# One product for two 16-key tiles in an attention's value products

## The chip, the cores and the metric

The kernel runs on one core of a Trainium2 chip. TensorE (PE) multiplies, VectorE (DVE) and ScalarE (ACT) do elementwise work, GpSimd (POOL) some sums and DMA issues, SyncE (SP) issues the loads of weights. The metric is the time of one execution in device microseconds.

## The reference

One layer of a hybrid decoder in float32: 512 tokens of 1024 features with 16 meta tokens in front (T = 528). Attention (16 heads of 64) and a causal convolution module (31 taps) read the same normalised input; their gated sum goes through an output projection, then come a squared-ReLU MLP and a last normalisation. The change touches only the attention:

```
logit[t,s] = q_t.k_s/sqrt(64) + sum_{s<j<=t} log f_j        (s <= t)
starts = [0] + list(range(16, 528, 128))
block [q0,q1) reads keys [0,q1):  p = softmax(s);  out = p @ v[:, :q1]
```

The outputs of the meta tokens' own block are dropped, so there are four query tiles of 128 queries, q = 0 to 3, with 144, 272, 400 and 528 keys.

## The kernel before

**Precision.** Every float32 operand of a large product is held as a high and a low part in float32r (`*_hi`, `*_lo`). A projection's chunk is 8 x 3 products (high by high, low by high, high by low). Its weights are copied to `w_hi` by ACT (L568) and the rest to `w_lo` by DVE (L940).

**Pairs and steps.** Heads are worked in 8 pairs. A pair takes 8 steps, `s` = 0 to 7; step `s` handles unit `s`: head `s // 4` of the pair and query tile `s % 4`. At the same time PE computes the next pair's four projections (v, gate, q, k; one chunk in two steps), so that the products of a chunk stand between the pieces of attention work. DVE fills its time with the taps of the convolution (L1035), a fixed number in each step (`TAPS_STEP`, 18 or 19 in a pair; pairs 5 to 8 have the extra one in step 4). The order on every engine is written out by hand (`pair_step`), engines meet by semaphores.

**A unit.** PE multiplies queries by keys into PSUM (`unit_scores`, L1544, L1545); DVE adds the mask, writes `prob` and takes the row's minimum (L1075); ACT exponentiates with a row sum (L657); DVE takes the reciprocal (L1081); ACT normalises `prob` in place (`normalise`, L665). One step later PE transposes `prob` in tiles of 128 keys (`unit_transpose`, L1558); ACT copies the result to `pt_hi` (L673, `probs_high`) and DVE the rest to `pt_lo` (L1087, `probs_low`). The transposes of a unit wait for the previous unit's low part (`s_ptl`) and for the unit's own normalisation (`s_pn`).

**Tiles of keys.** 144 + 128 q keys make q + 2 tiles, the last of which has 16 keys. It lies in `prob` in a cell of 128 columns whose other columns are zero (`pads`), so that it is transposed like the others; `v_hl`, v's transposed high and low parts, has five tiles, the fifth with 16 keys and zeros.

**Values.** After two units, `half_out` multiplies: v's tile is stationary, the transposed probabilities of two query tiles move, 256 columns. A half has query tiles 0 and 1 (half 0) or 2 and 3 (half 1). The last tile of the half's second query tile stands alone: its products have 128 columns (L1578), the others 256 (L1575). Half 0 is in steps 3 (head 0) and 7 (head 1), half 1 in step 5 and in step 1 of the next pair, each behind the transposes of its step. ACT's copy of unit 2 or 6 to `pt_hi` waits for half 0 (`s_pv`).

**v.** In step 3 ACT copies the next pair's v product to `vT` (L693), in the same step as it normalises unit 3; PE transposes `vT` in step 2 of the next pair and writes the PSUM of `vT`'s product again from step 4 on, for which it waits (`s_vev`).

Of the kernel before, what the change touches and what calls it, by code (L numbers as in the profile page):

```python
# [20 lines left out]
F32 = mybir.dt.float32  # L21
F32R = mybir.dt.float32r
ALU = mybir.AluOpType
ACT = mybir.ActivationFunctionType
AX_X = mybir.AxisListType.X

P = 128
D = 1024
KT = D // P
NT = 512  # L30
META = 16
T = NT + META
H = 16
HD = 64
PAIRS = H // 2
QT = NT // P
# [54 lines left out]
KT5 = QT + 1  # L91
VT = KT5 * P
SHORT_AT, LONG_AT = 0, 4 * P
FIRST_CELL = (0, 2, 0, 4)
CELLS = 9
N_F = 2
N_GLU = 1
N_PAIR = N_GLU + 2 * KT
# [26 lines left out]
def build(nc, x, meta_tokens, norm_mix_gain, w_in, b_forget, w_attn_out, b_glu, conv_dw_w, conv_dw_b,  # L125
# [3 lines left out]
    with ExitStack() as ctx:  # L129
        def sb(name, shape, dt=F32):  # L130
            return ctx.enter_context(nc.sbuf_tensor(name, shape, dt))

        def sem(name):
            return ctx.enter_context(nc.semaphore(name))
# [18 lines left out]
        ga = sb("ga", [P, KT * NT])  # L153

        in_hi = sb("in_hi", [P, KT * ROW], F32R)
        in_lo = sb("in_lo", [P, KT * ROW], F32R)

        with ExitStack() as pairs_only:  # L160
            k_a, k_b, q_a, q_b = (pairs_only.enter_context(nc.sbuf_tensor(name, [P, 2, 2, width], F32R))
                                  for name, width in (("k_a", T), ("k_b", T), ("q_a", NT), ("q_b", NT)))
            pt_hi, pt_lo = (pairs_only.enter_context(nc.sbuf_tensor(name, [P, CELLS * P], F32R))
                            for name in ("pt_hi", "pt_lo"))
            v_hl = pairs_only.enter_context(nc.sbuf_tensor("v_hl", [P, KT5, 2, P], F32R))
# [6 lines left out]
        pT = sb("pT", [P, 2, NT])  # L172
        sb("rest_pt", [P, 2 * CELLS * P - 2 * NT])
        xs_meta_t = sb("xs_meta", [P, D])
# [4 lines left out]
        vT = sb("vT", [P, VT])  # L179
        ident = sb("ident", [P, P])  # L180
# [1 line left out]
            d_lo = last_block.enter_context(nc.sbuf_tensor("d_lo", [P, KT * NT], F32R))  # L182
        u = sb("u", [P, KT * UW])
        prm = sb("prm", [P, KT * NR])
        ones = sb("ones", [P, 1])
        nmax = sb("nmax", [P, 8])
        rsum = sb("rsum", [P, 8])
        rinv = sb("rinv", [P, 8])
        eps_rms = sb("eps_rms", [P, 1])
        eps_ln = sb("eps_ln", [P, 1])  # L190
        bf = sb("bf", [H, 1])
        ss = sb("ss", [P, 2 * QT])
        sd = sb("sd", [P, QT + 1])
        rstd = sb("rstd", [P, QT + 1])
# [2 lines left out]
        pj = ctx.enter_context(nc.psum_tensor("pj", [P, 2, 1024], F32))  # L197
# [3 lines left out]
        pO7 = pQ[:, 1536:2048]  # L201
# [28 lines left out]
        def probs(q, first=0, last=None):  # L230

            end = LONG_AT if q % 2 == 0 else LONG_AT + VT
            at = end - (q + 2) * P
            return prob[:, at + first:end if last is None else at + last]

        def turned(q):

            at = 1024 - (P if q == QT - 1 else 0)
            return pQ[:, at:at + (q + 2) * P]

        def cells(buf, q):

            return buf[:, FIRST_CELL[q] * P:(FIRST_CELL[q] + q + 2) * P]

        def count(k, it=None, per=0):

            return k if it is None else it * per + k

        def wait(eng, signal, k, it=None, per=0):

            if it is None and k <= 0:
                return
            assert k > 0
            eng.wait_ge(signal, count(k, it, per))
# [5 lines left out]
        def feat(buf, m):  # L260
            return buf[:, ds(m * NT, NT)]
# [8 lines left out]
        AT = 512 - HALF  # L270

        def prod(c, width=NT):
            if width == T:
                return pj[:, c % 2, AT:AT + T]
            return pj[:, 0, 0:NT] if c % 2 == 0 else pj[:, 1, 512:512 + NT]

        HW = D // 2
        down_hi = (d_hi[:, :], in_hi[:, 0:KT * HW])  # L280
# [10 lines left out]
        def y_psum(t, f):  # L291

            return (pQ if f == 0 else pj[:, :, :].rearrange("p a b -> p (a b)"))[:, t * HW:(t + 1) * HW]
# [48 lines left out]
        s_vev = sem("s_vev")  # L342
# [14 lines left out]
        s_one = sem("s_one")  # L357
# [21 lines left out]
        s_pn = sem("s_pn")  # L379
# [181 lines left out]
        def _(act):  # L561
            A = nc.scalar.activation
# [97 lines left out]
            def normalise(s, k, it=None):  # L660

                U = 8 * k + s
                wait(act, s_rinv, U + 1, it, 16)
                nk = META + P * (s % QT + 1)
                A(probs(s % QT, 0, nk), probs(s % QT, 0, nk), ACT.Copy, scale=rinv[:, s:s + 1]).then_inc(s_pn, 1)  # L665

            def probs_high(s, k, it=None):

                U = 8 * k + s
                h, q = divmod(s, QT)  # L670
                wait(act, s_T, U + 1, it, 16)
                wait(act, s_pv, 4 * k + 2 * h + q // 2, it, 8)
                A(cells(pt_hi, q), turned(q), ACT.Copy).then_inc(s_pth, 1)  # L673
# [12 lines left out]
            def projection_out(s, k, it=None):  # L686

                c = N_PAIR + 4 * k + s // 2
                if s == 3:
                    if k == 0:  # L690
                        act.wait_ge(s_u, KT + 1)
                    wait(act, s_vl, k, it, 2)
                    A(vT[:, 0:T], prod(c - 1, T), ACT.Copy).then_inc(s_vev, 1)  # L693
                elif s % 2 == 0 and c > N_PAIR:
                    wait(act, s_mm, c, it, 8)
                    if s == 0:
                        A(feat(ga, count(k - 1, it, 2)), prod(c - 1), ACT.Copy).then_inc(s_gev, 1)
                    elif s in (4, 6):
                        dst, width, scale, done = (q_a, NT, -HD ** -0.5, s_qh) if s == 4 else (k_a, T, 1.0, s_kh)
                        for h in range(2):  # L700
                            A(dst[0:HD, k % 2, h, :], prod(c - 1, width)[h * HD:(h + 1) * HD, :], ACT.Copy,
                              scale=scale).then_inc(done, 1)
# [74 lines left out]
            for s in range(8):  # L777
                k = PAIRS
                c = N_PAIR + 4 * k + s // 2
# [14 lines left out]
            for k in (PAIRS + 1,):  # L794
                for s in range(8):
                    c = N_PAIR + 4 * k + s // 2
# [137 lines left out]
        def _(dve):  # L934
            V = nc.vector
# [20 lines left out]

            V.memset(f_one, 1.0).then_inc(s_one, 1)
            V.memset(vT[:, T:VT], 0.0).then_inc(s_one, 1)
            for cell in (3, 8):
                V.memset(pads[:, cell, META:P], 0.0).then_inc(s_pads, 1)  # L960
            V.memset(q_b[HD:HD + 2, :, :, :].bitcast(F32), -1.0).then_inc(s_one2, 1)
# [121 lines left out]
            def probs_low(s, k):  # L1083

                q = s % QT
                wait(dve, s_pth, 8 * k + s + 1)
                V.tensor_tensor(cells(pt_lo, q), turned(q), cells(pt_hi, q).bitcast(F32),  # L1087
                                ALU.subtract).then_inc(s_ptl, 1)
# [167 lines left out]
            for m in range(KT):  # L1256
                c = N_AO + m
# [11 lines left out]
            with dve.Fori(0, KT // 4) as it:  # L1269
                for j in range(4):  # L1270
                    m = it * 4 + j
                    c = N_CO + j
# [138 lines left out]
        def _(pe):  # L1411
            mm = nc.tensor.matmul
# [94 lines left out]
            for m in range(KT):  # L1507
                last = nc.tensor.transpose(pPrm[:, m * NR:(m + 1) * NR], prow[:, m * P:(m + 1) * P],
                                           ident[0:NR, 0:NR])
# [39 lines left out]
            def unit_transpose(s, k, it=None):  # L1549

                U = 8 * k + s
                q = s % QT
                wait(pe, s_pn, U + 1, it, 16)
                wait(pe, s_ptl, U, it, 16)
                if q == QT - 1 and U + 2 <= 8 * PAIRS:
                    wait(pe, s_max, U + 2, it, 16)
                for t in range(q + 2):
                    last = nc.tensor.transpose(turned(q)[:, t * P:(t + 1) * P], probs(q, t * P, (t + 1) * P), ident[:, :])  # L1558
                last.then_inc(s_T, 1)

            def half_out(h, half, k, it=None):

                q0 = 2 * half
                wait(pe, s_ptl, 8 * k + 4 * h + q0 + 2, it, 16)
                if half == 0:
                    wait(pe, s_vl, k + 1, it, 2)
                    wait(pe, s_ob, 2 * k + h, it, 4)
                dst = pO7[:, q0 * P:(q0 + 2) * P]
                for t in (0, q0 + 2, *range(1, q0 + 2)):
                    for part in (pt_hi, pt_lo):  # L1570
                        grid = part[:, :].rearrange("p (c n) -> p c n", n=P)
                        first, second = FIRST_CELL[q0] + t, FIRST_CELL[q0 + 1] + t
                        flags = dict(start=t == 0 and part is pt_hi, stop=t == q0 + 1 and part is pt_lo)
                        if t < q0 + 2:
                            last = mm(dst.rearrange("p (c n) -> p c n", n=P), v_hl[:, t, h, :],  # L1575
                                      grid[:, first:second + 1:second - first, :], **flags)
                        else:
                            last = mm(dst[:, P:2 * P], v_hl[:, t, h, :], grid[:, second, :], **flags)  # L1578
                last.then_inc(s_pv, 1)

            def values_transpose(k, it=None):
# [43 lines left out]

            pe.wait_ge(s_sig, KT + 1)
            pe.wait_ge(s_one2, 1)
            pe.wait_ge(s_one, 2)
            pe.wait_ge(s_pads, 2)
            for k in range(2):  # L1630
                for s in range(8):
# [20 lines left out]
            for n0, hi, lo, ready in ((N_AO, mid_hi, mid_lo, s_olo), (N_CO, in_hi, in_lo, s_clo)):  # L1652
                with pe.Fori(0, KT // 4) as it:
                    for j in range(4):
                        begin(n0 + j, it)
                        chunk(n0 + j, 0, total, hi, lo,
                              first=(lambda kt: pe.wait_ge(ready, kt + 1)) if j == 0 else None)
# [69 lines left out]
            for f in range(2):  # L1727
                for t in range(QT):
# [6 lines left out]
                    for kt in range(KT):  # L1735
# [4 lines left out]
                        for hidden, w, n in ((mid_hi, down_hi, 0), (mid_hi, down_lo, 1), (mid_lo, down_hi, 2)):  # L1740
                            last = mm(y_psum(t, f), hidden[:, tok], w[f][:, cols],  # L1741
                                      start=kt == 0 and n == 0, stop=kt == KT - 1 and n == 2)
# [29 lines left out]
```

## Time and profile before

| | us |
|---|---|
| three runs | 914.67, 916.97, 917.04 |
| median | 916.97 |
| the profiled execution | 913.51 |
| its span | 911.5 |
| PE, DVE, ACT busy in it | 901.0, 612.5, 443.7 |

The span runs from the first to the last instruction that the profiler recorded. Attention's eight pairs stand between about 135 and 405 us; before them are the convolution's gate projections, behind them the output projections and the MLP, in which PE does almost only products of 512 columns.

### The profile page before, as it was taken

What the parts mean: (1) busy time and instruction counts of PE and PEld (TensorE: products, weight loads), DVE (VectorE), ACT (ScalarE), POOL (GpSimd) and SP (SyncE); (2) the same over time, 40 slices, a digit from 0 to 9 for tenths busy, and PEclk for the clock granted to TensorE, in tenths of its full rate; (3) what the DMA queues carried; (4) which work ended last, traced back from release to release, by engine and by line L of the source; (5) the groups of instructions that cost most, each with busy time, mean ns of one, the idle gap of its engine ahead of it and who ended that gap; (6) DMA issues with size and microseconds to landing.
All of it is one profiled execution on the core that took longest, in us unless ns stands there. A gap on an engine that the chain in (4) does not pass through costs nothing.

```text
span 911.5 us, 13692 instructions
## 1 busy us (share of the span) xinstructions
PE 901.0 (99%) x5045; PEld 785.5 (86%) x5045; DVE 612.5 (67%) x956; ACT 443.7 (49%) x720; POOL 22.3 (2%) x40
## 2 busy tenths in 40 slices
PE   8999999999999999999999999999999999999997
PEld 7999998899999999888888888888888888888886
DVE  7699989999999999986766444533443354334543
ACT  6432246777778777766842244421243133214423
POOL 2010000000000000010000000000000000000000
PEclk9999999999999999999999999999999999999999
DMA  9333332212221222212323532333233332333502
GB/s 263 96 97 93 91 94 70 70 49 70 69 66 50 69 70 56 80 56 87 115 79 104 186 93 83 102 93 101 86 103 104 92 92 93 114 93 108 169 1 93
DMA packets 129466, 84.34 MB, mean 93 GB/s; under 512 B 3103, under 2 KB 118815, under 8 KB 129424
## 3 DMA queue, kind: packets, MB, share of 16 engines
q1 hardware_dynamic: 128192, 82.32, 30.9%
q10 hardware_dynamic: 640, 1.18, 0.4%
q8 instruction: 25, 0.41, 0.2%
q0 software_dynamic: 592, 0.29, 0.2%
q14 instruction: 17, 0.14, 0.0%
HBM read 81.62 MB, written 2.16 MB: 92 GB/s over the span
## 4 chain that ended last, share of the span: by engine, by line
PE 94%; DVE 3%; ACT 1%; issue 1%; DMA 1%; ACTq 0%; DVEq 0%
PE pj L1435 42%; PE pQ L1675 19%; PE pj L1431 17%; PE pQ L1558 3%; PE pQ L1575 3%; PE pj L1741 2%; PE pQ L1741 2%; PE pj L1473 1%; DVE cv L1035 1%; PE pQ L1545 1%; PE pQ L1544 1%; DVE w_lo L940 1%; PE pQ L1578 1%; DMA u<-in_norm_mix_gain_dram 1%; PE pQ L1452 1%
## 5 line engine op out<-in xcount | busy, mean ns | idle before, releaser
L940 DVE TENSOR_TENSOR w_lo<-raw,w_hi 128x1024 fp32r<-128x1024 f32 x129 | 157.7, 1222 | 114.6 <-ACT w_hi L568 114.2
L568 ACT ACTIVATE w_hi<-raw 128x1024 fp32r<-128x1024 f32 x129 | 135.9, 1053 | 161.4 <-PE pQ L1675 121.3
L1435 PE MATMUL pj<-in_hi,w_lo 128*128 128x512 f32 x512 | 201.5, 393 | 0.0
L1435 PE MATMUL pj<-in_lo,w_hi 128*128 128x512 f32 x512 | 200.7, 392 | 0.0
L1435 PE MATMUL pj<-in_hi,w_hi 128*128 128x512 f32 x512 | 200.6, 392 | 0.0
L1035 DVE SCALAR_TENSOR_TENSOR cv<-u,prm,cv 128x512 f32<-128x512 f32 x240 | 170.6, 745 | 0.5
L1435 PEld LDWEIGHTS pj<-in_hi,w_hi 128*128 128x128 f32 x512 | 96.3, 188 | 20.4 <-DVE w_lo L947 0.9
L1435 PEld LDWEIGHTS pj<-in_lo,w_hi 128*128 128x128 f32 x512 | 96.2, 188 | 18.0 <-issue 0.2
L1435 PEld LDWEIGHTS pj<-in_hi,w_lo 128*128 128x128 f32 x512 | 96.3, 188 | 17.1
L1675 PE MATMUL pQ<-w_hi,mid_hi 128*128 128x512 f32 x256 | 99.8, 390 | 0.0
L1675 PE MATMUL pQ<-w_lo,mid_hi 128*128 128x512 f32 x256 | 99.6, 389 | 0.0
L1675 PE MATMUL pQ<-w_hi,mid_lo 128*128 128x512 f32 x256 | 99.6, 389 | 0.0
L1431 PE MATMUL pj<-in_hi,w_lo 128*128 128x264 f32 x480 | 97.9, 285 | 0.0
L1431 PE MATMUL pj<-in_lo,w_hi 128*128 128x264 f32 x480 | 97.4, 284 | 0.0
L1431 PE MATMUL pj<-in_hi,w_hi 128*128 128x264 f32 x480 | 96.7, 283 | 0.4 <-ACT vT L693 0.4
L1431 PEld LDWEIGHTS pj<-in_hi,w_hi 128*128 128x128 f32 x480 | 74.9, 188 | 1.6 <-issue 0.7
L1431 PEld LDWEIGHTS pj<-in_lo,w_hi 128*128 128x128 f32 x480 | 74.0, 188 | 0.0
L1431 PEld LDWEIGHTS pj<-in_hi,w_lo 128*128 128x128 f32 x480 | 73.9, 188 | 0.0
L881 ACT ACTIVATE prob<-pT 128x512 f32<-128x512 f32 x32 | 20.2, 632 | 102.3 <-DVE pT L1326 102.3
L657 ACT ACTIVATE prob<-prob,nmax 128x144 f32<-128x144 f32 (+1 forms) x64 | 36.7, 573 | 42.0 <-DVE nmax L1075 42.0
L1675 PEld LDWEIGHTS pQ<-w_hi,mid_lo 128*128 128x128 f32 x256 | 48.1, 188 | 10.0
L1675 PEld LDWEIGHTS pQ<-w_lo,mid_hi 128*128 128x128 f32 x256 | 48.1, 188 | 10.0
(197 smaller groups left out, 1236.3 us busy)
## 6 DMA issues: line engine op xcount, KB each, us to landing
raw<-in_w_in_dram SPq DMA_DIRECT2D x57, 512.0 KB, 3.8
raw<-in_w_mlp_up_dram SPq DMA_DIRECT2D x32, 512.0 KB, 3.9
raw<-in_w_mlp_down_dram SPq DMA_DIRECT2D x32, 512.0 KB, 3.8
raw<-in_w_attn_out_dram SPq DMA_DIRECT2D x8, 512.0 KB, 3.6
raw<-in_w_conv_out_dram SPq DMA_DIRECT2D x8, 512.0 KB, 3.6
raw<-in_w_out_dram SPq DMA_DIRECT2D x8, 512.0 KB, 3.9
ga<-in_x_dram SPq DMA_DIRECT2D x4, 512.0 KB, 8.8
cv<-in_x_dram SPq DMA_DIRECT2D x1, 2048.0 KB, 9.1
```

Source lines behind the costliest of these rows:

```text
L568: A(w_hi[:, c % SPLIT, :], raw[:, c % RAW, :], ACT.Copy).then_inc(s_hi, 1)
L657: A(probs(s % QT, 0, nk), probs(s % QT, 0, nk), ACT.Exp, bias=nmax[:, s:s + 1], scale=-1.0, accum_out=rsum[:, s:s + 1]).then_inc(s_exp, 1)
L881: A(scratch(j), pT[:, j % 2, :], ACT.Square).then_inc(s_hf, 1)
L940: V.tensor_tensor(w_lo[:, c % SPLIT, :], raw[:, c % RAW, :], w_hi[:, c % SPLIT, :].bitcast(F32), ALU.subtract).then_inc(s_lo, 1)
L1035: V.scalar_tensor_tensor(out=dst, in0=src, scalar=par(j, m), in1=dst, op0=ALU.mult, op1=ALU.add).then_inc(s_conv, 1)
L1431: last = mm(prod(c, T)[:, h * HALF:(h + 1) * HALF], wt, src[:, kt * ROW + FIRST + h * HALF:kt * ROW + FIRST + (h + 1) * HALF], **flags)
L1435: last = mm(prod(c), wt, src[:, at:at + NT], **flags)
L1452: last = nc.tensor.transpose(in_psum(t)[:, m, :], src, ident[0:n, 0:n])
L1558: last = nc.tensor.transpose(turned(q)[:, t * P:(t + 1) * P], probs(q, t * P, (t + 1) * P), ident[:, :])
L1575: last = mm(dst.rearrange("p (c n) -> p c n", n=P), v_hl[:, t, h, :], grid[:, first:second + 1:second - first, :], **flags)
L1675: last = mm(y_psum(t, 0), mid[:, tok], w[:, c % SPLIT, cols], start=kt == 0 and n == 0, stop=kt == KT - 1 and n == 2)
L1741: last = mm(y_psum(t, f), hidden[:, tok], w[f][:, cols], start=kt == 0 and n == 0, stop=kt == KT - 1 and n == 2)
```

## The change

The lone tiles of query tiles 1 and 3 are multiplied together, one product for the high and one for the low part, in half 1. Both need one stationary operand, so the fifth tile of `vT` holds keys 256 to 271 in rows 0 to 15 and keys 512 to 527 in rows 32 to 47. Query tile 1's lone tile has its keys in rows 0 to 15 already; query tile 3's are put in rows 32 to 47, by normalising them into a new buffer `lone_probs` of 48 columns, 32 of them zero, from which the last transpose of the unit reads. The product takes 48 rows and moves 256 columns (cells 4 and 9 of `pt_hi` or `pt_lo`). `FIRST_CELL` gives query tile 3 cells 5 to 9, so that query tile 1's lone cell outlives the copies of units 2 and 3. The accumulation of a head is now started once, in half 0, for all four query tiles.

ACT's `normalise` has two instructions for query tile 3, and its copy of v has two. The new buffer takes free columns in front of the rows of `in_lo`; four one-column constants move into one tensor; DVE zeroes 32 columns more at the start.

```diff
...
 KT5 = QT + 1
 VT = KT5 * P
 SHORT_AT, LONG_AT = 0, 4 * P
-FIRST_CELL = (0, 2, 0, 4)
-CELLS = 9
+FIRST_CELL = (0, 2, 0, 5)
+CELLS = 10
+LONE_ROW = 32
 N_F = 2
 N_GLU = 1
 N_PAIR = N_GLU + 2 * KT
...
         ga = sb("ga", [P, KT * NT])
 
         in_hi = sb("in_hi", [P, KT * ROW], F32R)
+        with ExitStack() as row_gap:
+            lone_probs = row_gap.enter_context(nc.sbuf_tensor("lone_probs", [P, LONE_ROW + META], F32))
         in_lo = sb("in_lo", [P, KT * ROW], F32R)
 
 
...
             d_lo = last_block.enter_context(nc.sbuf_tensor("d_lo", [P, KT * NT], F32R))
         u = sb("u", [P, KT * UW])
         prm = sb("prm", [P, KT * NR])
-        ones = sb("ones", [P, 1])
         nmax = sb("nmax", [P, 8])
         rsum = sb("rsum", [P, 8])
         rinv = sb("rinv", [P, 8])
-        eps_rms = sb("eps_rms", [P, 1])
-        eps_ln = sb("eps_ln", [P, 1])
-        bf = sb("bf", [H, 1])
+        columns = sb("columns", [P, 4])
+        ones, eps_rms, eps_ln = (columns[:, i:i + 1] for i in range(3))
+        bf = columns[0:H, 3:4]
         ss = sb("ss", [P, 2 * QT])
         sd = sb("sd", [P, QT + 1])
         rstd = sb("rstd", [P, QT + 1])
...
             at = end - (q + 2) * P
             return prob[:, at + first:end if last is None else at + last]
 
+        def probs_cell(q, t):
+            return lone_probs[:, :] if (q, t) == (QT - 1, QT) else probs(q, t * P, (t + 1) * P)
+
         def turned(q):
 
             at = 1024 - (P if q == QT - 1 else 0)
...
             return pj[:, 0, 0:NT] if c % 2 == 0 else pj[:, 1, 512:512 + NT]
 
 
+
+        def lone_values(c):
+
+            at = AT + 2 * P
+            return pj[:, c % 2, at:at + 4 * P].rearrange("p (a b) -> p a b", b=2 * P)[:, :, 0:META]
 
         HW = D // 2
         down_hi = (d_hi[:, :], in_hi[:, 0:KT * HW])
...
                 U = 8 * k + s
                 wait(act, s_rinv, U + 1, it, 16)
                 nk = META + P * (s % QT + 1)
-                A(probs(s % QT, 0, nk), probs(s % QT, 0, nk), ACT.Copy, scale=rinv[:, s:s + 1]).then_inc(s_pn, 1)
+                last = A(probs(s % QT, 0, min(nk, NT)), probs(s % QT, 0, min(nk, NT)), ACT.Copy, scale=rinv[:, s:s + 1])
+                if nk > NT:
+                    last = A(lone_probs[:, LONE_ROW:], probs(s % QT, NT, nk), ACT.Copy,
+                             scale=rinv[:, s:s + 1])
+                last.then_inc(s_pn, 1)
 
             def probs_high(s, k, it=None):
 
...
                     if k == 0:
                         act.wait_ge(s_u, KT + 1)
                     wait(act, s_vl, k, it, 2)
-                    A(vT[:, 0:T], prod(c - 1, T), ACT.Copy).then_inc(s_vev, 1)
+                    A(vT[:, 0:NT], prod(c - 1, T)[:, 0:NT], ACT.Copy)
+                    A(vT[:, NT:VT].rearrange("p (a b) -> p a b", b=LONE_ROW)[:, 0:2, 0:META],
+                      lone_values(c - 1), ACT.Copy).then_inc(s_vev, 1)
                 elif s % 2 == 0 and c > N_PAIR:
                     wait(act, s_mm, c, it, 8)
                     if s == 0:
...
 
             V.memset(f_one, 1.0).then_inc(s_one, 1)
             V.memset(vT[:, T:VT], 0.0).then_inc(s_one, 1)
+            V.memset(lone_probs[:, 0:LONE_ROW], 0.0).then_inc(s_one, 1)
             for cell in (3, 8):
                 V.memset(pads[:, cell, META:P], 0.0).then_inc(s_pads, 1)
             V.memset(q_b[HD:HD + 2, :, :, :].bitcast(F32), -1.0).then_inc(s_one2, 1)
...
                 if q == QT - 1 and U + 2 <= 8 * PAIRS:
                     wait(pe, s_max, U + 2, it, 16)
                 for t in range(q + 2):
-                    last = nc.tensor.transpose(turned(q)[:, t * P:(t + 1) * P], probs(q, t * P, (t + 1) * P), ident[:, :])
+                    last = nc.tensor.transpose(turned(q)[0:probs_cell(q, t).shape[1], t * P:(t + 1) * P], probs_cell(q, t),
+                                               ident[:, :])
                 last.then_inc(s_T, 1)
 
             def half_out(h, half, k, it=None):
...
                 if half == 0:
                     wait(pe, s_vl, k + 1, it, 2)
                     wait(pe, s_ob, 2 * k + h, it, 4)
-                dst = pO7[:, q0 * P:(q0 + 2) * P]
-                for t in (0, q0 + 2, *range(1, q0 + 2)):
+                dst = pO7.rearrange("p (c n) -> p c n", n=P)
+                for t in (0, 1) if half == 0 else (0, QT, 1, 2, 3):
                     for part in (pt_hi, pt_lo):
                         grid = part[:, :].rearrange("p (c n) -> p c n", n=P)
-                        first, second = FIRST_CELL[q0] + t, FIRST_CELL[q0 + 1] + t
-                        flags = dict(start=t == 0 and part is pt_hi, stop=t == q0 + 1 and part is pt_lo)
-                        if t < q0 + 2:
-                            last = mm(dst.rearrange("p (c n) -> p c n", n=P), v_hl[:, t, h, :],
-                                      grid[:, first:second + 1:second - first, :], **flags)
+                        if t < QT:
+                            first, second = FIRST_CELL[q0] + t, FIRST_CELL[q0 + 1] + t
+                            last = mm(dst[:, q0:q0 + 2, :], v_hl[:, t, h, :], grid[:, first:second + 1:second - first, :],
+                                      start=half == 0 and t == 0 and part is pt_hi,
+                                      stop=t == QT - 1 and part is pt_lo)
                         else:
-                            last = mm(dst[:, P:2 * P], v_hl[:, t, h, :], grid[:, second, :], **flags)
+                            first, second = FIRST_CELL[1] + 2, FIRST_CELL[QT - 1] + t
+                            rows = LONE_ROW + META
+                            mm(dst[:, 1:QT:2, :], v_hl[0:rows, t, h, :], grid[0:rows, first:second + 1:second - first, :],
+                               start=False, stop=False)
                 last.then_inc(s_pv, 1)
 
             def values_transpose(k, it=None):
...
 
             pe.wait_ge(s_sig, KT + 1)
             pe.wait_ge(s_one2, 1)
-            pe.wait_ge(s_one, 2)
+            pe.wait_ge(s_one, 3)
             pe.wait_ge(s_pads, 2)
             for k in range(2):
                 for s in range(8):
```

## Rows read from the trace of the kernel before

**Rows 1.** The page: busy us (share, count) by engine; chain's shares
```profile
PE 901.0 (99%) x5045; PEld 785.5 (86%) x5045; DVE 612.5 (67%) x956; ACT 443.7 (49%) x720; POOL 22.3 (2%) x40
...
PE 94%; DVE 3%; ACT 1%; issue 1%; DMA 1%; ACTq 0%; DVEq 0%
```
**Rows 2.** Windows: stretch, its length, busy us by engine, clock, DMA
```profile
242.81:275.60 32.79, 32.79 (x230) 30.35 (x229) 30.79 (x63) 24.60 (x49) 1.81 (x2) 1.00 0.23 64
275.60:308.53 32.93, 32.93 (x230) 30.32 (x229) 31.34 (x64) 24.62 (x49) 1.83 (x2) 1.00 0.23 64
```
**Rows 3.** Groups by form: busy us, mean ns of one, idle before
```profile
L1575 PE MATMUL pQ<-pt_lo,v_hl 128*128 128x256 f32 x96 | 25.7, 282 | 0.0
...
L1578 PE MATMUL pQ<-pt_lo,v_hl 128*128 128x128 f32 x32 | 8.8, 275 | 0.0
...
L1578 PE MATMUL pQ<-pt_hi,v_hl 128*128 128x128 f32 x32 | 7.2, 224 | 0.0
```
**Rows 4.** Timeline of weight loads, step 3 of pair 4: start us, us
```profile
248.44 0.19 PEld L1575 LDWEIGHTS pQ<-pt_hi,v_hl 128*128 128x128 f32 x1
...
248.67 0.19 PEld L1578 LDWEIGHTS pQ<-pt_hi,v_hl 128*128 128x128 f32 x1
248.78 0.19 PEld L1578 LDWEIGHTS pQ<-pt_lo,v_hl 128*128 128x128 f32 x1
248.90 0.19 PEld L1575 LDWEIGHTS pQ<-pt_hi,v_hl 128*128 128x128 f32 x1
```
**Rows 5.** Timeline of PE where 48 stationary columns follow 128
```profile
27.32 0.64 PE L1473 MATMUL pj<-in_hi,w_lo 128*128 128x264 f32 x4
27.80 0.28 PE L1484 MATMUL pj<-in_hi,w_hi 128*48 128x264 f32 x1
```
**Rows 6.** Timeline of PE before unit 4's transposes: pairs 4, 5 and 1
```profile
255.83 0.41 PE L1431 MATMUL pj<-in_lo,w_hi 128*128 128x264 f32 x2
256.08 0.38 PE L1558 MATMUL pQ<-ident,prob 128*128 128x128 f32 x2
...
288.58 0.40 PE L1431 MATMUL pj<-in_lo,w_hi 128*128 128x264 f32 x2
288.90 0.41 PE L1558 MATMUL pQ<-ident,prob 128*128 128x128 f32 x2
...
157.60 0.41 PE L1558 MATMUL pQ<-ident,prob 128*128 128x128 f32 x2 [0.23 <-DVE pt_lo L1087]
```
**Rows 7.** Timeline of ACT, steps 3 and 4 of pair 4
```profile
248.18 0.59 ACT L693 ACTIVATE vT<-pj 128x528 f32<-128x528 f32 x1
248.67 0.72 ACT L665 ACTIVATE prob<-prob,rinv 128x528 f32<-128x528 f32 x1
249.45 0.60 ACT L673 ACTIVATE pt_hi<-pQ 128x512 fp32r<-128x512 f32 x1
249.94 1.05 ACT L568 ACTIVATE w_hi<-raw 128x1024 fp32r<-128x1024 f32 x1
```
**Rows 8.** Timeline of DVE, minima of steps 3 and 5, pair 4
```profile
246.69 0.71 DVE L1075 CUSTOM_DVE_ANT_0 prob<-pQ,mask 128x528 f32<-128x528 f32 x1 [0.75 <-PE pQ L1545]
...
254.58 0.44 DVE L1075 CUSTOM_DVE_ANT_0 prob<-pQ,mask 128x272 f32<-128x272 f32 x1 [0.46 <-PE pQ L1545]
```
**Rows 9.** Timeline of DVE: pair 5's steps 4 and 5, pair 1's step 4
```profile
286.12 1.41 DVE L1125 SCALAR_TENSOR_TENSOR q_a<-pj,q_a 64x512 fp32r<-64x512 f32 x2
287.57 0.44 DVE L1075 CUSTOM_DVE_ANT_0 prob<-pQ,mask 128x272 f32<-128x272 f32 x1
287.93 0.09 DVE L1075 DVE_READ_ACCUMULATOR2_ANT nmax<- 128x1 f32 x1
287.93 0.82 DVE L1087 TENSOR_TENSOR pt_lo<-pQ,pt_hi 128x640 fp32r<-128x640 f32 x1
...
153.98 0.16 DVE L1081 RECIPROCAL rinv<-rsum 128x1 f32<-128x1 f32 x1 [0.27 <-ACT prob L657]
```
**Rows 10.** Groups by form on ACT; PE's waits: us, times, longest
```profile
L665 ACT ACTIVATE prob<-prob,rinv 128x528 f32<-128x528 f32 x16 | 11.7, 733 | 2.2 <-DVE rinv L1081 2.2
...
L665 ACT ACTIVATE prob<-prob,rinv 128x144 f32<-128x144 f32 x16 | 6.5, 406 | 1.2 <-DVE rinv L1081 1.2
...
PE pj L1431 <- ACT vT L693: 0.4, 1, 0.4
```

## The prediction

> **What bounds the kernel now.** I read the page first. TensorE (PE) is busy for 901.0 of 911.5 us and holds 94% of the chain that ended last [rows 1]. The change lies in the attention pairs, so next come the windows of two of the eight pairs (each from one transpose of v to the next): PE is never idle, its clock is at full speed, VectorE (DVE) works 30.8 and 31.3 us of 32.8 and 32.9, ScalarE (ACT) 24.6 [rows 2]. So PE sets the pace, but DVE is close: a fraction of a microsecond saved on PE can turn into a wait for DVE. What I have to find is the price of the removed products on PE, and which waits of a pair have no slack.
>
> **The price of a product.** The durations of [rows 3] overlap and are no price; starts are. In the loads around the products of one half, that of the first lone product starts at 248.67, of the second at 248.78, of the next 256-wide one at 248.90 [rows 4]: 0.11 and 0.12 us each, so the lone pair takes 0.23 us. The 256-wide ones go at 0.12 (248.44 to 248.67 is two of them, 0.23). So a product of 128 columns costs as much as one of 256: the weight load in front of it (0.11 us apart at best) is what it pays for.
>
> **Part by part, PE.** Per head four products of 128 columns go (q1's and q3's, high and low part; 64 in all [rows 3], which shows 32 of either part) and two of 256 columns with 48 rows come. Removed 4 x 0.115 = 0.46, added 2 x 0.12 = 0.24: 0.22 us less per head, 16 heads, 3.5 us at most. By place: the first half of a head (in steps 3 and 7 of a pair) becomes 0.23 shorter, the second half (steps 5 and 1 of the next) 0.01 longer. That a product of 48 rows costs what one of 128 does is my value, since no row shows 48; the ends are 0.11 for each, the shortest spacing of [rows 4] (0.3 us more gain in all), and the rival with the drain below. The last transpose of query tile 3 now has 48 stationary columns, still 128 moving ones. Going from 128 to 48 stationary columns costs nothing in the start of the kernel: four products from 27.32 at 0.12 put the fourth at 27.68, and the first 48-column one starts at 27.80 [rows 5]. I take 0 for it; ends 0.05 us either way for each of 16 (half of the 0.11 of a load), so 0.8.
>
> **Part by part, ACT.** The normalisation of query tile 3 becomes two instructions (512 and 16 wide), 16 times; v's copy becomes two (512, and 2 x 16), 8 times. From 128x144 at 406 ns and 128x528 at 733 [rows 10], an element costs 0.85 ns and an instruction 284 ns fixed; 16 wide makes about 0.30 us. But v's copy (0.59 long) starts 0.49 before the instruction behind it, 248.18 to 248.67 [rows 7]: about 0.10 of each duration overlaps. So a tail costs ACT 0.20 us, less the 0.014 taken from the wide part: 0.19; for v's, reading PSUM, I take 0.10. Ends: 0 and 0.30 for each. Total about 3.8 us of ACT's, which works 24.6 of 32.8, so only its place matters.
>
> In step 3 the order is exponential, v's copy, normalise(3), then the high copy of unit 2's turned probabilities, then w_hi, q's copies, exponential(4) and its row sum, on which DVE's reciprocal waits. Now normalise(3) starts at 248.67 and the copy behind at 249.45, 0.78 later, though 0.62 would do (0.72 less 0.10) [rows 7]: 0.16 is a wait for the first half's products, which will end 0.23 sooner. Tails of 0.29 less 0.16 leave ACT about 0.13 late from there to the reciprocal (ends 0 and 0.4).
>
> **What PE's saving then meets.** Steps 3 to 5 are the tight place. DVE starts from step 3's scores after idling 0.75, and works through to step 5's row minimum, behind which stands the low part of unit 3, on which unit 4's transposes on PE wait.
> - Pairs 2 to 4 (such as the one at 242.81): DVE idles 0.46 before step 5's minimum [rows 8], and PE starts the transposes 0.25 after the last but one product, 255.83 to 256.08 [rows 6], the ordinary spacing of two 264-wide products. PE 0.23 earlier and DVE 0.13 later make 0.36 of 0.46: it fits. Saving 2 x 0.22 per pair, three pairs: 1.3 us.
> - Pairs 5 to 7 have one conv tap more in step 4. DVE goes from there into the minimum at 287.57 without idling [rows 9], and PE waits: 288.58 to 288.90 is 0.32, 0.07 over the ordinary [rows 6]. The first head's 0.22 is lost whole, and ACT's 0.13 comes on top; the second head's 0.22 stays (the chain has 0.75 idle in front of the next step 3, of which 0.22 goes). 0.09 per pair, 0.3 us.
> - Pair 1: PE idles on DVE's low part already, at 157.60 [rows 6], and in its step 4 DVE waits for ACT 0.27, at 153.98 [rows 9], so the whole 0.29 of the tails comes through. Its second head saves 0.22: net -0.07.
> - Pair 8 has no q and v left to cast and no such wait that I see: 0.44.
> - PE waits once for v's copy, 0.4 us, in the first step [rows 10]: a longer copy adds 0.1.
>
> In step 7 the tail of normalise(7) delays exponential and reciprocal of the next step by 0.2; DVE takes that from its 0.75. Memsets at the start stand beside DMA waits; the merged constants and the shifted buffers cost nothing (DVE and PE do not touch them differently). SP's and POOL's queues get nothing new, and the new value of PE's start wait is long reached.
>
> Sum: 1.3 + 0.3 - 0.1 + 0.4 - 0.1 = 1.9 us (with all rounding, ends 0 and 3.5). The profiled execution took 913.51 us for a span of 911.5: it would become 911.6. The three runs go from 914.67 to 917.04, median 916.97; the sum taken from the median gives 915.1, and I say 915.0, since the profiled execution and one run lie below.
>
> **A rule weighed.** That the load, not the columns, prices the lone products is what the starts show [rows 4]. The Trainium skill, "TensorEngine Tiling (Array Packing)", Key Properties, speaks against the change: in its words "Mode switching requires drain", and it gives row tiling for contractions of at most 64 rows, where these have 48. In columns, this trace does not agree ([rows 5], 0.12 us across the switch). In rows, no run here shows it yet; it is the second rival.
>
> **The rivals.**
> 1. All is kept. The waits in steps 4 and 5 turn out looser (the tails on ACT nearly free, DVE's order giving way elsewhere). For it: the waits that I see are under 0.1 us each in pairs 5 to 7. Against: an engine without idle time cannot move up. Gain 3.5: 913.5.
> 2. A change of rows drains PE. A product's result lasts 282 ns [rows 3] and the next starts 0.12 after it; if the array must be empty before 48-row weights act, and again after, each of two changes per head costs 0.28 - 0.12 = 0.16, 32 of them 5.2 us. 5.2 - 1.9 = 3.3 slower: 920.3. It decides from 0.06 us per change on. For it: nothing of these rows shows 64 rows or fewer beside full products without a wait. Against: 128 to 48 columns is free [rows 5]. Place: the loads of the two 48-row products, in steps 5 and 1.
> 3. ACT's tails are dear (0.3 each, not hidden). The copy behind them comes 0.6 - 0.16 = 0.44 late. Pairs 2 to 4 then wait too, 0.23 + 0.44 - 0.46 = 0.21 each, and still save 0.23 (0.7 in all); pairs 5 to 7 lose 0.22 each (0.7), pair 1 loses 0.4, pair 8 saves 0.4, the first step loses 0.3. In sum about 0: 917.0. For it: a tail is almost all fixed cost. Against: the overlap of 0.10 is seen behind every ACT row of [rows 7].
>
> **Chances.** Forecast (gain 1 to 2.9) 0.53; rival 1 0.18; rival 3 0.15; rival 2 0.12; other 0.02. What a measurement can tell from no change is 0.3%, 2.75 us. Faster by more than that: rival 1 nearly whole, a tenth of the forecast's, and scatter of the median: 0.27. Slower: rival 2 mostly, 0.11. Within: 0.62. The range goes from 912.4 (3.5 gained, and a median 1 us low) to 918.0 (rival 3 with a median 1 us high); rival 2 is left out.
>
> **What would show it.** In the profile after: 32 products of 256 columns with 48 rows in place of 64; starts 0.12 apart around them (0.28 would be rival 2); first halves 0.23 shorter; pairs 2 to 4 about 32.35 us long, pairs 5 to 7 about 32.85; PE's wait before unit 4's transposes in pairs 5 to 7 about 0.4 us instead of 0.07; DVE's idle 0.46 fallen to 0.1; the tail on ACT 0.30 us long. I am wrong if pairs 5 to 7 shorten as much as 2 to 4 (rival 1), or if all of them lengthen.

## The result and the profile after

The changed kernel is slower: 917.81 us (median of 15 runs, 917.45 to 920.67) against 914.56 for the kernel before, run beside it (15 runs, 913.14 to 917.04). The ratio is 1.0037, 95% interval 1.0027 to 1.0048. In most kernels here some runs, with a mean granted clock of 0.992 to 0.994 instead of 0.996 to 1.000, take 2 to 4 us longer, so that a median also depends on how many of them it holds. The forecast was 915.0 with most of the chance on "within 0.3%"; what came has the sign and the size of its second rival (3.3 us slower), the size in part by luck (see the part on why the prediction was wrong). The profiled execution took 918.48 us with a span of 916.5, 5.0 us over the span before; about 0.6 of that is there before the first unit's transposes. In the first 15 us TensorE (PE) waits for the first inputs (0.7 us for DVE cv and 1.3 for xs_meta, 0.4 and 0.8 before) and its granted clock is 0.89, 1.00 before; this start differs by up to 1 us between the kernels here.

The page, busy us by engine and the chain's shares, answering to [rows 1]:

```profile
PE 903.9 (99%) x5013; PEld 783.4 (85%) x5013; DVE 613.6 (67%) x957; ACT 446.4 (49%) x744; POOL 22.3 (2%) x40
...
PE 91%; DVE 4%; ACT 3%; issue 1%; DMA 1%; ACTq 0%; DVEq 0%
```

32 products less, and yet PE's time is longer: what has grown lies between products. DVE and ACT have gained shares of the chain. The windows of pairs 4 and 5 against [rows 2] put 0.39 and 0.63 us on a pair, with the clock still at full speed:

```profile
245.07:278.25 33.18, 33.18 (x227) 30.14 (x226) 30.91 (x63) 24.92 (x52) 1.82 (x2) 1.00 0.23 64
278.25:311.81 33.56, 33.34 (x227) 30.15 (x226) 31.54 (x64) 24.94 (x52) 1.84 (x2) 1.00 0.23 63
```

The weight loads of a second half (step 5 of pair 4), to be read by their starts, as [rows 4]:

```profile
258.30 0.19 PEld L1592 LDWEIGHTS pQ<-pt_lo,v_hl 128*128 128x128 f32 x1
258.63 0.18 PEld L1598 LDWEIGHTS pQ<-pt_hi,v_hl 48*128 48x128 f32 x1
258.74 0.19 PEld L1598 LDWEIGHTS pQ<-pt_lo,v_hl 48*128 48x128 f32 x1
259.06 0.19 PEld L1592 LDWEIGHTS pQ<-pt_hi,v_hl 128*128 128x128 f32 x1
```

Here is the loss. The first load with 48 rows starts 0.33 behind the load before it, the second 0.11 behind the first, and the first with 128 rows again 0.32 behind: the ordinary spacing is 0.11 to 0.12. All 16 second halves show the same, 0.32 or 0.33 at either change. A change of rows, in either direction, costs about 0.2 us. The timeline of PE shows the same from the side of the products: starts 0.21 and 0.22 apart, in place of 0.12, though the products are of the ordinary width:

```profile
258.42 0.28 PE L1592 MATMUL pQ<-pt_lo,v_hl 128*128 128x256 f32 x1
258.63 0.38 PE L1598 MATMUL pQ<-pt_hi,v_hl 48*128 48x256 f32 x1
258.85 0.28 PE L1598 MATMUL pQ<-pt_lo,v_hl 48*128 48x256 f32 x1
```

The groups by form show it only on the first product behind a change: the high part's with 48 rows is 382 ns long, the low part's 277, beside 281 for the low part's with 128 rows and [rows 3]. The two tails on ScalarE (ACT), the short second instructions, are the others of the new rows:

```profile
L1598 PE MATMUL pQ<-pt_hi,v_hl 48*128 48x256 f32 x16 | 6.1, 382 | 0.0
L677 ACT ACTIVATE lone_probs<-prob,rinv 128x16 f32<-128x16 f32 x16 | 4.7, 295 | 0.0
...
L1598 PE MATMUL pQ<-pt_lo,v_hl 48*128 48x256 f32 x16 | 4.4, 277 | 0.0
...
L708 ACT ACTIVATE vT<-pj 128x32 f32<-128x32 f32 x8 | 1.5, 186 | 0.0
```

The second loss is the one that the prediction had for pairs 5 to 7. PE before unit 4's transposes in pair 5, as [rows 6]: the last but one product starts at 291.00, the transposes at 291.62, 0.62 instead of 0.32, and the ordinary is 0.25:

```profile
291.00 0.40 PE L1448 MATMUL pj<-in_lo,w_hi 128*128 128x264 f32 x2
291.62 0.41 PE L1575 MATMUL pQ<-ident,prob 128*128 128x128 f32 x2 [0.22 <-DVE pt_lo L1104]
```

And PE's waits, of which v's copy has grown from [rows 10]:

```profile
PE pQ L1575 <- DVE pt_lo L1104: 1.1, 4, 0.4
PE pj L1448 <- ACT vT L708: 0.7, 1, 0.7
```

### The profile page after: what moved, and what is told of

The parts are those of the page before. It is cut to its first block, busy times and chain, and to the rows that moved or that the text cites. A ratio compares the mean times of both kernels' runs of the same rounds, so it can differ in the third digit from the quotient of the medians.

```text
span 916.5 us, 13653 instructions
## 1 busy us (share of the span) xinstructions
PE 903.9 (99%) x5013; PEld 783.4 (85%) x5013; DVE 613.6 (67%) x957; ACT 446.4 (49%) x744; POOL 22.3 (2%) x40
## 4 chain that ended last, share of the span: by engine, by line
PE 91%; DVE 4%; ACT 3%; issue 1%; DMA 1%; ACTq 0%; DVEq 0%
PE pj L1452 41%; PE pQ L1696 19%; PE pj L1448 15%; PE pQ L1592 3%; PE pj L1762 2%; PE pQ L1762 2%; PE pQ L1575 2%; PE pj L1490 1%; DVE cv L1052 1%; PE pQ L1562 1%; PE pQ L1561 1%; PE pQ L1598 1%; ACT w_hi L578 1%; DVE w_lo L956 1%; DMA u<-in_norm_mix_gain_dram 1%
```

## The experiments

Each kernel ran beside the kernel before on the same chip, in three sets (medians of that 913.8 to 913.9). The changed kernel was in none of them, so a difference in us from its 917.81, or between two sets, can be off by some tenths; the ratios are each to the kernel before beside it. The letters A to E name theories: A is that a change of rows empties PE; the others are told in the expectations.

**All 128 rows.** The joined product stays; only its rows change.

```diff
-                            rows = LONE_ROW + META
+                            rows = P
```

> The changed kernel with all 128 rows in the two joint products (rows 48 to 127 of v's fifth tile are zero). Theory A, a change between products of 128 rows and of 48 empties TensorE: in the changed trace the load of the first 48-row product starts 0.32 us behind the load before it instead of 0.12, and so does the first 128-row one behind them, 0.20 us each, 32 times, 6.5 us. Then this kernel loses them: second halves at the ordinary spacing (10 products in about 1.18 us instead of 1.56), time 911.3 to 913.5, that is about 2 us under the kernel before, as the prediction's sum without its rival said. Theory B, the loss is in ScalarE's two tails and the waits behind them: time stays at about 917.8.

Measured 912.44 us, ratio 0.9984 (0.9974 to 0.9993). By the medians 5.4 us came back from one number. From the first unit's transposes to the last unit's PE takes 258.18 us before, 262.10 in the changed kernel and 256.44 here: 5.7 us for the 30 changes between, 0.19 for each. The same place in step 5 of pair 4, weight loads:

```profile
256.30 0.19 PEld L1592 LDWEIGHTS pQ<-pt_lo,v_hl 128*128 128x128 f32 x1
256.42 0.19 PEld L1598 LDWEIGHTS pQ<-pt_hi,v_hl 128*128 128x128 f32 x1
256.54 0.19 PEld L1598 LDWEIGHTS pQ<-pt_lo,v_hl 128*128 128x128 f32 x1
256.65 0.19 PEld L1592 LDWEIGHTS pQ<-pt_hi,v_hl 128*128 128x128 f32 x1
```

Both gaps are gone. Windows of pairs 4 and 5:

```profile
242.88:275.30 32.42, 32.42 (x227) 29.94 (x226) 30.85 (x63) 24.86 (x52) 1.81 (x2) 1.00 0.23 65
275.30:308.16 32.86, 32.66 (x227) 29.98 (x226) 31.38 (x64) 24.83 (x52) 1.83 (x2) 1.00 0.23 64
```

The prediction gave 32.35 and 32.85 for them, and 1.9 us for the whole, of which 1.7 came by the stretch above and 1.45 by the medians. So its sum holds for this kernel, and theory B falls.

**80 and 64 rows.** The same line with `rows = 80` and `rows = 64`.

> The same with 80 rows. Theory A with the limit at 64 rows (the part of the array that a product takes is counted in halves or wholes): no gap, as with 128 rows, 911.3 to 913.5. Theory A with a gap for any number of rows other than 128: loads 0.32 apart, 917.8. (The products with 66 rows in the scores show 0.12 and speak for the first.)

> The same with 64 rows. Theory A with the limit at 64 rows: gaps as with 48 rows, time as the changed kernel, 917.3 to 918.5. If 64 rows cost nothing: 911.3 to 913.5.

80 rows: 911.88 us, ratio 0.9978 (0.9966 to 0.9989). 64 rows: 917.90 us, 1.0048 (1.0032 to 1.0063). The loads of the joined products, 80 rows first, then 64:

```profile
256.37 0.19 PEld L1592 LDWEIGHTS pQ<-pt_lo,v_hl 128*128 128x128 f32 x1
256.50 0.19 PEld L1598 LDWEIGHTS pQ<-pt_hi,v_hl 80*128 80x128 f32 x1
```

```profile
257.54 0.19 PEld L1592 LDWEIGHTS pQ<-pt_lo,v_hl 128*128 128x128 f32 x1
257.87 0.18 PEld L1598 LDWEIGHTS pQ<-pt_hi,v_hl 64*128 64x128 f32 x1
```

0.13 against 0.33. Somewhere above 64 and at or below 66 rows the gap ends: the scores' products of 66 rows stand between full ones without it, 0.13 and 0.12 apart (step 3 of pair 5, 80-row kernel):

```profile
278.83 0.19 PEld L1561 LDWEIGHTS pQ<-k_a,q_a 128*128 128x128 f32 x1
278.96 0.19 PEld L1562 LDWEIGHTS pQ<-k_b,q_b 66*128 66x128 f32 x1
279.08 0.19 PEld L1452 LDWEIGHTS pj<-in_lo,w_hi 128*128 128x128 f32 x1
```

**The two products apart.** The order within a second half is changed, nothing else.

```diff
-                for t in (0, 1) if half == 0 else (0, QT, 1, 2, 3):
-                    for part in (pt_hi, pt_lo):
+                order = [(t, part) for t in ((0, 1) if half == 0 else (0, 1, 2, 3)) for part in (pt_hi, pt_lo)]
+                if half == 1:
+                    order.insert(2, (QT, pt_hi))
+                    order.insert(5, (QT, pt_lo))
```

> The changed kernel with the two 48-row products of a head apart: high part, then the two 128-row products of v's second tile, then the low part. Theory A, the price is paid at each change of rows: four changes per head instead of two, 32 more of 0.20 us, 6.4 us more than the changed kernel, about 924. Theory C, the price belongs to each 48-row product (it or its load is slow in itself): no difference, 917.8.

Measured 923.87 us, ratio 1.0115 (1.0096 to 1.0134), 6.1 over the changed kernel by the medians and 5.6 by the profiled spans (922.1 against 916.5). Step 5 of pair 4, weight loads; 0.33, 0.31, then 0.32 and 0.32:

```profile
260.09 0.19 PEld L1595 LDWEIGHTS pQ<-pt_lo,v_hl 128*128 128x128 f32 x1
260.42 0.18 PEld L1601 LDWEIGHTS pQ<-pt_hi,v_hl 48*128 48x128 f32 x1
260.73 0.19 PEld L1595 LDWEIGHTS pQ<-pt_hi,v_hl 128*128 128x128 f32 x1
260.84 0.19 PEld L1595 LDWEIGHTS pQ<-pt_lo,v_hl 128*128 128x128 f32 x1
261.16 0.18 PEld L1601 LDWEIGHTS pQ<-pt_lo,v_hl 48*128 48x128 f32 x1
261.48 0.19 PEld L1595 LDWEIGHTS pQ<-pt_hi,v_hl 128*128 128x128 f32 x1
```

As many products of 48 rows, twice as many changes, twice the gaps. The price is that of the change (A), not of the product (C).

**48 rows in the kernel before.** No joining, no tails, no new layout.

```diff
-                            last = mm(dst[:, P:2 * P], v_hl[:, t, h, :], grid[:, second, :], **flags)
+                            last = mm(dst[:, P:2 * P], v_hl[0:48, t, h, :], grid[0:48, second, :], **flags)
```

> The kernel before with its four lone products of a head taking 48 rows (16 hold keys, the others are zero) in place of 128, nothing else. Theory A: each of the two lone pairs of a head is a change and a change back, 64 changes at 0.205 us, 13 us more, about 927; the lone products stay 128 columns wide, so the price has nothing to do with joining two tiles. If the gap came from the joined product with its strided output: no difference, 914.

Measured 924.01 us, ratio 1.0113 (1.0094 to 1.0132): 10.2 us, not 13. The price of a change is confirmed without the joined product; its size was wrong on one side. Step 3 of pair 4:

```profile
252.34 0.19 PEld L1575 LDWEIGHTS pQ<-pt_lo,v_hl 128*128 128x128 f32 x1
252.66 0.18 PEld L1578 LDWEIGHTS pQ<-pt_hi,v_hl 48*128 48x128 f32 x1
252.77 0.19 PEld L1578 LDWEIGHTS pQ<-pt_lo,v_hl 48*128 48x128 f32 x1
253.03 0.19 PEld L1575 LDWEIGHTS pQ<-pt_hi,v_hl 128*128 128x128 f32 x1
```

Into the 48 rows it takes 0.32, out of them 0.26. Behind a product of 256 columns the load comes 0.21 late, behind one of 128 columns 0.15. It looks as if a load that changes the rows waits until the product in front of it is through, and a shorter one is through sooner: in the kernel before the product behind a 128-column one starts 0.06 after it (248.78 to 248.84 on PE), the one behind a 256-column one 0.12, the same 0.06 less. The wait itself is in no row, since the recorded ends of products are modelled. 32 x (0.21 + 0.15) = 11.5, near the 10.2 (10.5 by the spans, 922.0 against 911.5).

**The tails alone.** In the kernel before, query tile 3's normalisation and v's copy are cut in two.

```diff
-                A(probs(s % QT, 0, nk), probs(s % QT, 0, nk), ACT.Copy, scale=rinv[:, s:s + 1]).then_inc(s_pn, 1)
+                last = A(probs(s % QT, 0, min(nk, NT)), probs(s % QT, 0, min(nk, NT)), ACT.Copy, scale=rinv[:, s:s + 1])
+                if nk > NT:
+                    last = A(probs(s % QT, NT, nk), probs(s % QT, NT, nk), ACT.Copy, scale=rinv[:, s:s + 1])
+                last.then_inc(s_pn, 1)
...
-                    A(vT[:, 0:T], prod(c - 1, T), ACT.Copy).then_inc(s_vev, 1)
+                    A(vT[:, 0:NT], prod(c - 1, T)[:, 0:NT], ACT.Copy)
+                    A(vT[:, NT:T], prod(c - 1, T)[:, NT:T], ACT.Copy).then_inc(s_vev, 1)
```

> The kernel before with nothing but ScalarE's two more instructions: query tile 3's normalisation in 512 and 16 columns, v's copy in 512 and 16. Theory D, the tails push VectorE's chain of steps 3 to 5: PE waits 0.13 us more before unit 4's transposes in each of pairs 5 to 7, 0.2 to 0.3 more in pair 1, 0.3 more for v's copy in the first step, in all about 0.9 us, 0.1%. Theory E, the waits of the changed kernel come from the shorter first halves alone: only the 0.3 of the first step.

Measured 916.28 us, ratio 1.0021 (1.0009 to 1.0033), 1.9 us by the ratio; its trace shows 0.8 us (span 912.3), 0.5 of it between the first and the last unit's transposes. PE before unit 4's transposes in pair 5:

```profile
288.98 0.40 PE L1435 MATMUL pj<-in_lo,w_hi 128*128 128x264 f32 x2
289.38 0.41 PE L1562 MATMUL pQ<-ident,prob 128*128 128x128 f32 x2
```

0.40 where the kernel before had 0.32 [rows 6]: 0.08 more, I had said 0.13. In pair 1 the wait there grew by 0.18 (0.41 after 0.23), as expected; the wait for v's copy grew by 0.07 (0.46 after 0.39), not by 0.3. Theory D holds, at about half the size. The median's 1.9 us is not the tails' price: 6 of the 12 runs have a granted clock of 0.992 to 0.994, against 4 of the 35 of the kernel before, and the medians of the others are 914.35 and 913.76, 0.6 apart.

**No tails.** The 80-row kernel with one instruction for each again; the 16 keys are not moved.

> The 80-row kernel without the tails: the normalisation and v's copy are one instruction each as before, and the last transpose reads the cell as before. It leaves the move of the 16 keys into rows 32 to 47 out. Theory D: PE's wait before unit 4's transposes in pairs 5 to 7 is about 0.29 us over the ordinary spacing instead of 0.39 (0.07 plus the 0.22 that PE came earlier), pair 1 and the first step fall back to what they were, pair 8 has no wait; about 1 us less than with 80 rows, 910.9. Theory E: 0.39 stays.

Measured 911.23 us, ratio 0.9980 (0.9970 to 0.9989); by the medians 0.65 less than with 80 rows, inside both intervals. The traces tell them apart: from the first to the last unit's transposes 255.33 us and 256.57, 1.2 less for about 1 expected. The kernel without tails, then the one with 80 rows, at the same place of pair 5:

```profile
287.42 0.40 PE L1442 MATMUL pj<-in_lo,w_hi 128*128 128x264 f32 x2
287.84 0.41 PE L1569 MATMUL pQ<-ident,prob 128*128 128x128 f32 x2
```

```profile
288.31 0.40 PE L1448 MATMUL pj<-in_lo,w_hi 128*128 128x264 f32 x2
288.93 0.41 PE L1575 MATMUL pQ<-ident,prob 128*128 128x128 f32 x2 [0.22 <-DVE pt_lo L1104]
```

0.42 and 0.62. Beside them, from the ACT timelines of the same pair, the time from the start of v's copy to the start of the `pt_hi` copy behind the first half:

| pair 5, us | ACT, v's copy to `pt_hi` | PE, last but one product to transposes |
|---|---|---|
| before | 1.24 | 0.32 |
| tails alone | 1.35 | 0.40 |
| 80 rows, no tails | 1.12 | 0.42 |
| 80 rows, with tails | 1.37 | 0.62 |

Alone, the tails make 0.08 and PE's earlier coming 0.10 (0.22 expected); together they make 0.30, so their prices do not add up. ACT's `pt_hi` copy waits for the first half. When the half ends sooner and there are no tails, ACT starts that copy 0.12 sooner, VectorE (DVE) follows, and about half of the 0.22 is given back; the expectation had left this out. With the tails ACT is 0.13 late instead, as the prediction said.

**The tap moved.** Step 2 takes the extra tap of pairs 5 to 8 from step 4, in the 80-row kernel.

```diff
-TAPS_STEP = {18: (3, 4, 1, 2, 1, 2, 3, 2), 19: (3, 4, 1, 2, 2, 2, 3, 2)}
+TAPS_STEP = {18: (3, 4, 1, 2, 1, 2, 3, 2), 19: (3, 4, 2, 2, 1, 2, 3, 2)}
```

> The 80-row kernel with the extra convolution tap of pairs 5 to 8 in step 2 instead of step 4. If VectorE's order in step 4 is what costs PE the 0.39 in pairs 5 to 7: that wait falls to 0.15 or less, 0.7 to 1.0 us less, about 911.1. Rival: VectorE then comes late to step 3's row minimum, the wait moves to unit 2's transposes, and nothing is gained.

Measured 911.88 us, ratio 0.9978 (0.9967 to 0.9988): by the medians as with 80 rows, by the profiled spans 1.0 less (909.9 against 910.9). Pair 5 fell from 32.84 to 32.43 us, but a new wait stands in pair 8, before unit 58's transposes (from 377.50 to 378.26, where a 512-wide product takes 0.23):

```profile
377.50 0.39 PE L1452 MATMUL pj<-in_lo,w_hi 128*128 128x512 f32 x1
378.26 0.63 PE L1575 MATMUL pQ<-ident,prob 128*128 128x128 f32 x4 [0.38 <-DVE pt_lo L1104]
```

**The tail on GpSimd**, with the tap moved:

```diff
...
+            def lone_scale(U):
+
+                s = U % 8
+                pool.wait_ge(s_rinv, U + 1)
+                nc.gpsimd.tensor_scalar(lone_probs[:, LONE_ROW:], probs(QT - 1, NT, T), rinv[:, s:s + 1], None,
+                                        ALU.mult).then_inc(s_lone, 1)
...
```

> The same, and the 16-column tail of the normalisation on GpSimd, which is idle, instead of ScalarE. If the tail's 0.2 us on ScalarE counts: 0.3 to 0.6 us less than the kernel with the moved tap alone, about 910.6. Rival: GpSimd takes over 1 us from the reciprocal to its result and holds unit 3's or 7's transposes, or slows VectorE: 911.1 or more.

Measured 913.05 us, ratio 0.9990 (0.9979 to 1.0002): 1.2 us more than with the moved tap alone (the intervals just touch), 1.6 by the spans. An instruction of 16 columns is recorded with 1.3 us there, and the convolution's sums, the last of which I had queued behind the last of them, came late: PE waited 1.9 us for one. The rival's number came, by a place that it did not name (POOL's timeline, PE's waits):

```profile
265.62 1.32 POOL L560 TENSOR_SCALAR lone_probs<-prob,rinv 128x16 f32<-128x16 f32 x1 [2.26 <-DVE rinv L1104]
```

```profile
PE pQ L1675 <- POOL conv_sum L554: 1.9, 1, 1.9
```

**The tap moved in pairs 5 to 7 only**, in the 80-row kernel and in the kernel before:

```diff
-                steps = TAPS_FIRST_PAIR if k == 1 else TAPS_STEP[len(late) // 2]
+                steps = (TAPS_FIRST_PAIR if k == 1 else (3, 4, 2, 2, 1, 2, 3, 2) if 5 <= k <= 7
+                         else TAPS_STEP[len(late) // 2])
```

> The 80-row kernel with the extra tap in step 2 for pairs 5 to 7 only; pair 8 keeps it in step 4. In the trace of the kernel with the tap moved in all four pairs, pairs 5 to 7 lost their wait (32.4 us each instead of 32.85), but PE waited 0.53 us before unit 58's transposes in pair 8. If that is the moved tap's doing it goes: 0.4 to 0.5 us less than there, about 911.4. Rival: the wait belongs to the later arrival of something else in pair 8 and stays.

> The kernel before with the same moved tap and nothing else. If the moved tap helps only where PE comes earlier: it wins 3 x 0.07 and part of the 0.1 before unit 6's transposes, under 0.5 us, 913.5. If step 4 had been a loss in itself: 1 us or more.

The first: 910.73 us, ratio 0.9963 (0.9951 to 0.9976), the fastest of all, 3.1 us under the kernel before. The second: 913.84 us, ratio 1.0000 (0.9990 to 1.0009). By itself the moved tap is worth nothing that the medians show; in its trace pairs 5 to 7 take 98.1 us in all for 98.6 before. Once PE comes earlier it is worth more: those three take 97.1 in the first kernel, 98.5 with 80 rows alone. Window of pair 5 of the first:

```profile
275.19:307.56 32.37, 32.37 (x227) 29.91 (x226) 31.48 (x64) 24.84 (x52) 1.84 (x2) 1.00 0.23 65
```

## Why the prediction was wrong

1. **The step that failed** is the first term: "That a product of 48 rows costs what one of 128 does is my value". The product does; the change to it and back does not. I had the alternative priced (0.16 per change, 32 of them, 5.2 us) and gave it 0.12, because the switch to 48 stationary columns was free [rows 5]. That row is about columns of the weights and says nothing on rows. Measured: 0.20 to 0.21 per change in the loads, 0.19 in the length of the attention, 6 us or a little more in all. The prediction also said that no run showed such a change of rows. The trace before has one, in the constants' transposes at the start, which take 38 rows: their first load starts 0.31 behind the last one with 128 rows, where 0.11 is the spacing of the loads before. A wait of PE for a transfer stands between, so it is no clean reading, but it has the size of the gap that came:

```profile
12.79 0.14 PEld L1452 LDWEIGHTS pQ<-ident,cv 128*128 128x128 f32 x1
13.10 0.14 PEld L1508 LDWEIGHTS pj<-ident,u 38*128 38x128 f32 x1 [0.17 <-issue]
```

The Trainium skill, "TensorEngine Tiling (Array Packing)", Key Properties, says that a change of tiling mode drains the engine. The runs agree in that there is a price, with the limit between 64 rows (gap) and 66 (none), 0.21 us behind 256 columns and 0.15 behind 128; that the engine drains is not shown itself. With that statement and no row against it a chance of 0.12 was too low.
2. **The saving on PE was right.** First halves: 6 loads in about 0.69 us became 4 in 0.46. With 128 rows the second halves have no gap, and pairs 4 and 5 took 32.42 and 32.86 us for forecasts of 32.35 and 32.85. The printed terms of the prediction's sum add up to 1.8; unrounded they are 1.86. Those of its third rival give 0.3 us slower rather than 0.
3. **What the saving meets was right in place, and roughly in size.** Pairs 2 to 4 did not wait (DVE's idle 0.46 fell to 0.14, q's last low part ending at 256.44, the minimum starting at 256.58), pairs 5 to 7 did: 0.37 over the ordinary spacing, for about 0.4 forecast. Its two parts came as forecast too, PE 0.22 early and ACT 0.13 late; together they added 0.30, not 0.35. What the prediction missed is a wait in pair 8: the changed kernel comes 0.17 later to the first unit's transposes there.

```profile
255.03 1.41 DVE L1142 SCALAR_TENSOR_TENSOR q_a<-pj,q_a 64x512 fp32r<-64x512 f32 x2
256.58 0.44 DVE L1092 CUSTOM_DVE_ANT_0 prob<-pQ,mask 128x272 f32<-128x272 f32 x1
```

4. **The tails** are 0.295 and 0.186 us long. The first costs ACT 0.18 (0.81 from `normalise` to the next instruction, 0.63 without tails), for 0.19 forecast, v's 0.07 (0.56 where 0.49 was), for 0.10. PE's wait for v's copy grew by 0.3, not 0.1, but not for the tail: it is 0.39 before, 0.46 with the tails alone, 0.64 with 80 rows and no tails, 0.70 in the changed kernel. Most of it is the first half's saving, which PE loses again at once in this wait; the prediction had left that out. ACT's instruction behind the 16-wide one starts 0.20 after it (251.57 and 251.77), as forecast:

```profile
250.96 0.72 ACT L675 ACTIVATE prob<-prob,rinv 128x512 f32<-128x512 f32 x1
251.57 0.30 ACT L677 ACTIVATE lone_probs<-prob,rinv 128x16 f32<-128x16 f32 x1
251.77 0.59 ACT L687 ACTIVATE pt_hi<-pQ 128x512 fp32r<-128x512 f32 x1
```

5. **The transpose with 48 columns** cost nothing, as said: the 128-row kernel, which has it, shows the forecast periods.
6. **The sum of it.** 6.4 us of gaps in the second halves (16 x 0.40), less 3.6 in the first (16 x 0.22), 0.9 in pairs 5 to 7, about 0.2 each in pairs 1 and 8, 0.3 for v's copy make 4.4 us of the 5.0 between the two profiled spans; most of the rest is the start. The medians differ by 3.3, since the execution profiled before was among the faster of its kind and the one after among the slower; the fastest runs differ by 4.3 (917.45 and 913.14).
7. **Luck.** 917.81 lies inside the stated range, 912.4 to 918.0, although the mechanism behind the range failed. The range was built on 916.97, the median of three runs; fifteen runs give 914.56. From there the forecast is 912.7 and the range ends at 915.6. The rival's 3.3 us also came out closer than its parts: its changes were priced at 5.2 and cost about 6, and six of the fifteen runs before took 915.8 us or more, which keeps that median high.

## What to carry to other kernels

A product that touches only part of PE's rows is not a cheaper product: at 48 and at 64 rows, between products of 128, each change cost nearly as much as two ordinary small products. Zero rows were free (80 and 128 rows cost the same); take them along. And when an engine with no idle time is sped up, look at once for the engine that was nearly as busy: here one tap moved by two steps was worth half a microsecond at most before the change and took more than a microsecond of waits away after it.

## What the runs showed of the hardware

- Between products of 128 rows and of 48 or 64 rows the next load starts 0.31 to 0.33 us behind the last instead of 0.11 to 0.12, in both directions, when the product in front has 256 columns; with 80 rows 0.13. Behind a product of 128 columns it is 0.26.
- Two products of 48 rows in a row have their loads the ordinary 0.11 apart: between them nothing is paid.
- Products of 128 and of 256 columns, each with a load of 128 float32r columns, cost the same: the loads come 0.11 to 0.12 us apart with either.
- GpSimd is recorded with 1.3 us to scale 16 columns, ACT with 0.295.
